# Output products of a two-layer encoder step: each 512-column matmul issued as two of 256 columns

## The reference

```
y = concat([mixer_out, cross_out]) * silu(gate)
x = x + y @ w_out[l]          # w_out[l] is 1024 x 1024
```

## Time and profile before

| what | value |
|---|---|
| three executions | 2377.99, 2379.43, 2380.56 us |
| span of the profiled execution, first to last instruction | 2376.1 us |
| TensorE matmul busy | 2312.2 us (97%) in 23787 matmuls |
| TensorE weight load busy | 2094.7 us (88%) in 23787 loads |
| VectorE busy | 1819.5 us (77%) |
| ScalarE busy | 1413.5 us (59%) |
| GpSimd busy | 381.0 us (16%) |

### The profile page before, as it was taken

How to read it: one execution, slowest core, us unless ns; L and a number is a source line. 1 busy time by engine, 2 the same in 40 slices (tenths; PEclk the granted TensorE clock), 3 DMA queues, 4 the chain that set the end, 5 groups by cost and what they waited for, 6 DMA issues and landing times. The chain is left out here.

```text
span 2376.1 us, 61711 instructions
## 1 busy us (share of the span) xinstructions
PE 2312.2 (97%) x23787; PEld 2094.7 (88%) x23787; DVE 1819.5 (77%) x3555; ACT 1413.5 (59%) x3281; POOL 381.0 (16%) x585
## 2 busy tenths in 40 slices
PE   7999999999989999999999999999999989999998
PEld 4999999999967888888887999999999978888886
DVE  7889788887666656666666998797888777888885
ACT  4564666755565555555554564776757566666664
POOL 2332000000022221211112332000000112112111
PEclk9999999999999999999999999999999999999999
DMA  6886887769894222222226897886879793444442
GB/s 227 298 299 219 301 281 231 247 220 332 232 307 121 83 66 89 90 69 83 73 81 232 272 303 242 256 275 214 266 248 312 230 269 117 129 131 122 137 135 70
DMA packets 396664, 469.64 MB, mean 198 GB/s; under 512 B 39860, under 2 KB 248556, under 8 KB 396376
## 3 DMA queue, kind: packets, MB, share of 16 engines
q1 hardware_dynamic: 379832, 406.02, 54.4%
q0 software_dynamic: 14704, 54.92, 6.6%
q10 hardware_dynamic: 1840, 4.75, 0.7%
HBM read 318.77 MB, written 151.56 MB: 198 GB/s over the span
## 5 line engine op out<-in xcount | busy, mean ns | idle before, releaser
L1468 PE MATMUL pj_acc<-x_lo,pj_wh 128*128 128x256 f32 (+1 forms) x3080 | 780.9, 284 | 0.0
L1468 PE MATMUL pj_acc<-x_hi,pj_wh 128*128 128x256 f32 (+1 forms) x3080 | 780.8, 284 | 0.0
L1468 PEld LDWEIGHTS pj_acc<-x_hi,pj_wh 128*128 128x128 f32 x3080 | 578.4, 188 | 0.0
L1468 PEld LDWEIGHTS pj_acc<-x_lo,pj_wh 128*128 128x128 f32 x3080 | 578.4, 188 | 0.0
L509 ACT ACTIVATE pj_wh<-pj_wt 128x512 fp32r<-128x512 f32 x676 | 420.3, 634 | 255.9 <-DMA pj_wt<-tsum 175.1
L516 DVE SCALAR_TENSOR_TENSOR pj_wl<-pj_wt,pj_wh 128x512 fp32r<-128x512 f32 x676 | 467.0, 708 | 87.0 <-ACT pj_wh L509 79.3
L1464 PE MATMUL pj_acc<-x_hi,pj_wl 128*128 128x256 f32 (+1 forms) x3080 | 509.4, 287 | 13.8 <-DVE pj_wl L516 11.9
L1464 PEld LDWEIGHTS pj_acc<-x_hi,pj_wl 128*128 128x128 f32 x3080 | 425.3, 188 | 22.1 <-DVE pj_wl L516 19.5
L1307 DVE TENSOR_TENSOR pj_out<-pj_out,pj_acc 128x512 f32<-128x512 f32 (+1 forms) x448 | 320.8, 716 | 103.3 <-PE pj_acc L1468 69.7
L2541 DVE COPY pb_pt<-pb_SCTP 128x256 f32<-128x256 f32 (+2 forms) x266 | 115.8, 435 | 147.5 <-PE pb_SCTP L2352 74.3
L2676 ACT ACTIVATE pb_se<-pb_se,pb_mn 128x640 f32<-128x640 f32 (+4 forms) x208 | 154.6, 745 | 114.6 <-DVE pb_mn L2524 114.3
(11 more groups left out here) (371 smaller groups left out, 3992.1 us busy)
## 6 DMA issues: line engine op xcount, KB each, us to landing
pj_wt<-tsum SPq DMA_DIRECT2D x546, 256.0 KB, 3.8
proj<-pj_out SPq DMA_DIRECT2D x112, 512.0 KB, 4.2
tsum<-pj_wt SPq DMA_DIRECT2D x140, 256.0 KB, 3.2
pj_wraw<-in_w_in_dram POOLq DMA_DIRECT2D x24, 1024.0 KB, 6.6
tsum<-pj_wraw SPq DMA_DIRECT2D x56, 256.0 KB, 4.2
hg_x<-x_mid SPq DMA_DIRECT2D x17, 512.0 KB, 3.7
pb_gate<-proj SPq DMA_DIRECT2D x16, 512.0 KB, 5.1
pb_x<-in_x_prompt_dram SPq DMA_DIRECT2D x16, 512.0 KB, 3.8
```

The lines of the kernel that those rows point to most:

```text
L1468: ins = nc.tensor.matmul(BANK[j][:, 0:n], w.hi[j][:, k], x.of(y, p, j)[:, k], start=False, stop=(k == 3 and i == 1))
```

## The change

Each matmul of 512 columns in the two `project` functions becomes two of 256 columns, into the first and the second half of the same PSUM bank. Both take the same stationary block. The clearing flag (`start`) stays with the first matmul of a half, the closing flag and the semaphore with the last. In layer 0 the two follow each other; so do they in layer 1, where the two semaphore waits stay where they were.

```
                         if job == 0 and part == 0 and half == 0:
                             pe.wait_ge(s_wl, FIRST.index(group_of(0, k)) + 1)
-                        cs = slice(half * 512, half * 512 + 512)
-                        ins = nc.tensor.matmul(sum_of(job, half), (yl if part == 2 else yh)[job % 2][:, k],
-                                               (wol if part == 1 else woh)[:, group_of(job, k), cs],
-                                               start=(k == 0 and part == 0), stop=(k == KD - 1 and part == 2))
+                        for at in (0, 256):
+                            cs = slice(half * 512 + at, half * 512 + at + 256)
+                            ins = nc.tensor.matmul(sum_of(job, half)[:, at:at + 256], (yl if part == 2 else yh)[job % 2][:, k],
+                                                   (wol if part == 1 else woh)[:, group_of(job, k), cs],
+                                                   start=(k == 0 and part == 0 and at == 0), stop=(k == KD - 1 and part == 2 and at > 0))
...
                         if s % 4 == 0:
                             pe.wait_ge(s_yh, 2 * job + s // 4 + 1)
-                        cs = slice(half * 512, half * 512 + 512)
                         g = GROUPS[s]
-                        nc.tensor.matmul(to[:], yh[:, s], woh[:, g, cs], start=(s == 0), stop=False)
-                        nc.tensor.matmul(to[:], yh[:, s], wol[:, g, cs], start=False, stop=False)
+                        quarters = [(slice(at, at + 256), slice(half * 512 + at, half * 512 + at + 256)) for at in (0, 256)]
+                        for at, cs in quarters:
+                            nc.tensor.matmul(to[:, at], yh[:, s], woh[:, g, cs], start=(s == 0 and at.start == 0), stop=False)
+                        for at, cs in quarters:
+                            nc.tensor.matmul(to[:, at], yh[:, s], wol[:, g, cs], start=False, stop=False)
                         if s % 4 == 0:
                             pe.wait_ge(s_yl, 2 * job + s // 4 + 1)
-                        ins = nc.tensor.matmul(to[:], yl[:, s], woh[:, g, cs], start=False, stop=(s == KD - 1))
+                        for at, cs in quarters:
+                            ins = nc.tensor.matmul(to[:, at], yl[:, s], woh[:, g, cs], start=False, stop=(s == KD - 1 and at.start > 0))
```

## The result

The kernel after the change takes 2392.11 us (median, 2389.59 to 2394.86) against 2379.99 us before, measured in turns with it: ratio 1.0045, 95% interval 1.0031 to 1.0060. Predicted were 2377.5 us, a range of 2372.5 to 2382, and "the same". The profiled execution has a span of 2393.1 us at a granted clock of 0.997, as before the change, so the clock doesn't explain it.

The account below looks back on a forecast made before the run. TensorE's own stream was taken to bound both stages. Gain 10.6 less 7.8 at stretch starts is 2.8; less 0.4 absorbed and 0.5 for instructions, 1.9 us off the 2376.1 span; with 3.3 carried over, 2377.5 us, range 2372.5 to 2382.

Parts of the forecast that it names:

- steady cost: Output matmuls in long streams: two narrow take 0.2267 us against 0.2331 for one wide, at most 10.6 us gained.
- What bounds the kernel: Attention and recurrence stages: TensorE's own stream sets the time, so time saved per output matmul comes off nearly whole.
- Cost at the start of a stretch: 389 stretches of output matmuls, mostly behind transposes: narrow ones pay 0.020 us more each, 7.8 us in all.
- surcharge: What narrow matmuls pay more at the start of each stretch: taken as 0.020 us, between about 0.015 and 0.035.
- direct reading: Six narrow matmuls behind transposes, read from the trace: 0.79 us against 0.78 for a stretch of three wide.
- Instructions: Added instructions make about 13 more blocks, 6 or 7 in the recurrence stage: 0.5 us slower, bounds -4.9 and +4.9.
- Share of blocks that stall unchanged: Recurrence stage: the same share of instruction blocks stalls as before, so stalls grow 10%, 0.5 us.
- Absorbed by the waits for ScalarE: Recurrence stage, state updates behind stretches of nine: what those stretches save is waited for, 0.4 us.
- (b): Every pair: fixed price per added matmul and load, up to 10.8 us; slower from a 0.0029 us price up; chance 0.08.
- (c): Instruction blocks fall badly: the stalls double, 2381.9 us; chance 0.09.
- (a): Steady gain everywhere, no narrow surcharge at stretch starts: 2369.7 us, or 2373.6 with half the surcharge; chance 0.18.

Follow-up runs that it names:

- Experiment 9: Kernel with narrow matmuls in layer 1 only, y of layer 1 moved 32 bytes; ratio to the kernel before 1.0032 (1.0018 to 1.0046).
- experiments 4 and 5: Kernel before and kernel after, each with 64 tiny transposes before recurrence: 1.0032, 1.0050; then wide kernel before with twelve satisfied waits per block in layer 1: 1.0080.

## Why the prediction was wrong

The step that failed is the steady cost, and behind it the price of the instructions. Term by term: the matmuls were to save 2.8 us and cost 5.7 (3.1 in the attention stage, 2.6 in the recurrence), the instructions were to cost 0.5 and cost 5.9. That is 8.5 and 5.4 us; less the 0.4 that waits were to absorb, it is the miss of 13.5 between -1.9 and +11.6.

*What bounds the kernel*: right. The whole difference, 3.1 us in the attention stage and 8.5 in the recurrence (means of the table), went to the end: 11.6 against 12.1 in the medians, within what the untouched stages vary.

*Steady cost*: this term failed, in its sign. It was worked out as -0.0065 us a pair with 0.1133 from the earlier trace rows, and is +0.0029 to +0.0035: 0.236 to 0.2366 a pair against 0.2331. The rows were right, the transfer was not. The price of a matmul of this form depends on where its two operands start against each other, and the projection's tiles lie 192 bytes apart modulo 256, the output product's 224 (layer 1), 32 or 0 (layer 0, by job). Experiment 9 puts y at 192 and gets back the predicted 0.2267 in the last job and most of the shorter stretches. The stage then takes 424.9 us without its stalls, against 425.9 before (425.2 in the wide mean): the loss is gone and the medians by stretch add up to a gain of 1.1 us, less than the 2.7 predicted for this stage; a third of the steps still run at 0.118. The warning was in the trace of before too: the projection has stretches at 0.1178, and they were not looked for.

*Cost at the start of a stretch*: +0.012 us in the mean for a stretch of three, where "nothing, perhaps loses 0.01" was said. 256 such stretches are the 3.1 us of the attention stage. Three pairs at +0.0029 are 0.009 of it, so most is the steady term over again and the surcharge itself, 0.020, was taken too large. The prediction contradicted itself here: its direct reading (0.79 us against 0.78) times 256 is 2.6 us slower, near the truth, while its sum put the attention stage at nothing.

*Instructions*: the count was right, the price not. +0.5 us stood for it, with +4.9 as bound; the stalls are 5.9 us more on average, and even 9.2 in the one pair of traces that was timed first. "Share of blocks that stall unchanged" is what failed. The stage has 68 blocks after and 61 before, and of their ends 43 and 42 fall into the levels of small matmuls, so hardly more of them stand there; but 14 of these stalled after and 7 before, and outside the levels 5 against 1. Four of the five are in the output products themselves (L3047, L3051), whose rows now pass in half the time: the "slow stretches" are less slow. Why more of the block ends stall isn't shown. The number of instructions, their places and the narrow matmuls all changed together, and experiments 4 and 5 separate them only in part. The Trainium skill ("Runtime: NRT & Kernel Launch", Instruction fetch mechanics) has a block's crossing mostly hidden. Here 49 of the 68 are hidden, and the 19 others cost 14.3 us.

*Absorbed by the waits for ScalarE*: the mechanism was right and worked on a loss. The weight loads of the state updates waited 3.6 us in 9 places before and 0.3 in 2 after (0.2 to 0.4 in all narrow kernels at 224). The stretch of nine in front of them went from 2.29 us to 2.25 in the mean, while the other stretch of nine grew by 0.03 in the median.

*Rivals*: (b), a fixed price for each added matmul and load, is nearest in size: 5.7 us outside the stalls (3.1 + 2.6) over 1632 is 0.0035 each, above its point of 0.0029. Of its reason, one half is borne out (the excess belongs to the operands) and the other not: a price paid once per instruction would not go away when y is moved, and it does. (c), stalls nearly doubled, happened (7.5 to 13.4 in the means). The two together are the result, and the prediction gave no case in which both hold. (a) is refuted: the steady gain isn't there.

The rule of the Trainium skill's page "TensorE: Matmul & The Clock Gate" (Back-to-back issue gap), columns at 2.4 GHz and 2.5 ns, gives 4.1 us, which comes near the 5.7 measured outside the stalls by accident: its 215.8 and 109.2 ns lie below every placement measured (226.7 and 113.3 at best).

## What to carry to other kernels

The price of a matmul from one stage is not its price in another: before a 3% difference is multiplied by a thousand, look for the same form at its slow pace too, and compare the start addresses of the two operands modulo 256 bytes. Here a pad of 32 bytes is worth 0.0050 us for 256 columns and one of 224 bytes 0.0064 for 512 in a long stream, as much for each as the change was meant to bring; over the kernel, where most stretches are short, neither version was measurably faster than before. Splitting matmuls also costs instructions, and in a stage with dense runs of tiny matmuls the stalls at block ends can grow by more than the matmuls cost; read the stalls marked "issue" as a function of where blocks end. Two shifts by 128 rows moved them by some 3 us here.

## What the runs showed of the hardware

A 256-column fp32r matmul with its load costs 0.1133 to 0.120 us by placement, one of 512 columns 0.2267 to 0.2335, one of 128, 192 or 240 columns 0.1115 to 0.1117. The values multiplied, the bank, the order of halves and the reload of a stationary block made no difference. At a difference of 192 bytes there are two stable paces, 113.3 and 117.8 ns, in the projection with the same tiles. In the kernel after, a stall at a block's end lasts until 2.2 to 2.7 us after its fetch began; why some fetches begin so late is not settled, nor why difference 0 is best at 512 columns and worst at 256.
